# Feed-forward block of a hybrid decoder step on one core: sample rows' high and low parts in one operand, the last two down projections adjacent, and the first weight split moved into the block before

## The reference, cut to what matters

```python
def conv_ffn(hn, conv_buf, p):
    up = hn @ p['w_up']                      # 1024 -> 2 * 2816
    padded = jnp.concatenate([conv_buf.astype(up.dtype), up], axis=1)
    cw = p['conv_w']                         # causal, width 3, over positions
    c = p['conv_b'] + sum(cw[i] * padded[:, i:i + L] for i in range(CONV_W))
    gate, val = jnp.split(c, 2, axis=-1)
    return (jax.nn.silu(gate) * val) @ p['w_down'], padded[:, -(CONV_W - 1):]
...
    h = h + cross_attention(rmsnorm(h, p['norm_x']), mkv, p)
    f, new_conv = conv_ffn(rmsnorm(h, p['norm_ffn']), conv_buf, p)
    return h + f, new_kv, h_re, h_im, new_conv
```

## Time and profile before

| what | value |
|---|---|
| time, median of 3 runs | 2151.79 us (2150.81 to 2152.84) |
| time of the profiled execution | 2154.55 us |
| its span, first to last instruction | 2152.9 us |
| mean granted TensorE clock | 0.896 of full speed |
| PE matmul busy | 1995.6 us (93% of the span) |
| VectorE, ScalarE, GpSimd busy | 965.4, 671.2, 244.8 us |

### The profile page before, as it was taken

The page is one execution under the profiler, slowest core; times in us unless marked ns, Lnnn a source line. Parts: engine busy times, 40 slices in busy tenths (PEclk is TensorE's granted clock), DMA queues, the critical chain, the costliest instruction groups (busy, mean ns, idle before and its releaser), DMA issues. The chain is left out here.

```text
span 2152.9 us, 32099 instructions
## 1 busy us (share of the span) xinstructions
PE 1995.6 (93%) x12704; PEld 1856.9 (86%) x12704; DVE 965.4 (45%) x2020; ACT 671.2 (31%) x1575; POOL 244.8 (11%) x561
## 2 busy tenths in 40 slices
PE   5899999976999599899899898999999999999997
PEld 4798999866789499899899897989988998899886
DVE  5614445447021643644352126355455545554554
ACT  5324333322131532544342104322322232223221
POOL 2502505125100100000000000000000000000000
PEclk9999999955555699999997698999999999999998
DMA  4211100012213242220323310221211121112102
GB/s 139 62 38 43 45 17 21 7 58 89 41 51 106 74 159 69 69 89 1 93 79 104 107 40 20 62 59 32 60 30 58 32 60 30 57 32 60 30 21 82
DMA packets 135728, 125.24 MB, mean 58 GB/s; under 512 B 15284, under 2 KB 128080, under 8 KB 135602
## 3 DMA queue, kind: packets, MB, share of 16 engines
q1 hardware_dynamic: 129986, 109.28, 16.6%
q0 software_dynamic: 5632, 14.44, 2.1%
HBM read 112.43 MB, written 10.60 MB: 57 GB/s over the span
## 5 line engine op out<-in xcount | busy, mean ns | idle before, releaser
L2419 PE MATMUL bank<-XH,WH 128*128 128x352 f32 x1056 | 343.7, 326 | 0.0
L2419 PE MATMUL bank<-XL,WH 128*128 128x352 f32 x1056 | 339.6, 322 | 0.0
L2419 PE MATMUL bank<-XH,WL 128*128 128x352 f32 x1056 | 339.4, 321 | 0.0
L1899 PE MATMUL bank<-WH,XH 128*128 128x256 f32 (+1 forms) x864 | 250.7, 290 | 22.5 <-DVE WL L1795 22.5
L1899 PE MATMUL bank<-WL,XH 128*128 128x256 f32 (+1 forms) x864 | 246.8, 286 | 0.0
L1899 PE MATMUL bank<-WH,XL 128*128 128x256 f32 (+1 forms) x864 | 245.4, 284 | 0.0
L627 PE MATMUL bank<-WH,XH 128*128 128x256 f32 (+3 forms) x648 | 211.5, 326 | 7.7 <-DVE WL L433 7.7
L2350 DVE TENSOR_TENSOR hres<-hres,bank 128x512 f32<-128x512 f32 (+1 forms) x198 | 135.7, 685 | 176.4 <-PE bank L2443 176.2
L627 PE MATMUL bank<-WL,XH 128*128 128x256 f32 (+3 forms) x648 | 203.9, 315 | 0.0
L627 PE MATMUL bank<-WH,XL 128*128 128x256 f32 (+3 forms) x648 | 202.6, 313 | 0.0
L2419 PEld LDWEIGHTS bank<-XH,WH 128*128 128x128 f32 x1056 | 199.2, 189 | 1.2
(11 more groups left out here) (440 smaller groups left out, 3433.8 us busy)
## 6 DMA issues: line engine op xcount, KB each, us to landing
wstage<-w_up SPq DMA_DIRECT2D x44, 512.0 KB, 5.1
ring<-cache_mem_kv SPq DMA_DIRECT2D x64, 256.0 KB, 2.9
dstage<-w_down POOLq DMA_DIRECT2D x22, 512.0 KB
wstage<-w_in SPq DMA_DIRECT2D x10, 1024.0 KB, 5.0
ringS<-cache_kv_dil SPq DMA_DIRECT2D x16, 512.0 KB, 6.9
wstage<-w_xkv SPq DMA_DIRECT2D x8, 1024.0 KB, 5.4
ringS<-cache_kv_dil SPq DMA_DIRECT2D x48, 128.0 KB, 2.7
xin<-x_prompt SPq DMA_DIRECT2D x8, 512.0 KB, 3.5
```

Source lines behind the costliest of these rows:

```text
L1899: ins = nc.tensor.matmul(MM[s % 3][:r, 0:WB], x[:, k, cols], w[:, b % 2, k], start=k == 0 and i == 0, stop=k == KT - 1 and i == 2)
L2419: ins = nc.tensor.matmul(bank[3 * g + j][:, 0:CH], w[:, slot, k, P * g:P * g + P], x[:, k, CH * j:CH * j + CH], start=k == 0 and i == 0, s ...
```

## The change

It has four parts. (1) In `block_dense` "x", the split of the first `w_up` tile into `WH[:, 0]` and `WL[:, 0]` is done at step 32 of 36 (`up_at`) instead of at the start of the feed-forward block; there TensorE starts with the up projection, and the first parameters are transposed after two thirds of its first half. (2) The sample rows' high and low parts of a tile lie side by side in `AS` (64 columns). One matmul with 64 stationary columns and `DH` gives high x high on rows 0 to 31 and low x high on rows 32 to 63; a second, 32 wide, adds high x low. The two row groups are kept apart in `hres` (rows 32 to 63 of the ninth tile) and added once (`fold`) before the last down projection, which is done as before. (3) The parameters of both tiles of a pair lie in one 80-row tile and take one transpose, the last columns of both tiles lie in one 72-column tile and take one transpose. (4) In turn 10 the down projection of pair 9 is moved behind the up projection of tile 21, so that those of pairs 9 and 10 follow each other; the activations and `w_down` parts of tiles 20 and 21 go into the `WH`/`WL` slots that their own up projections have finished with.

```diff
+    up_at = None if has_m else STEPS - 4
...
+            def split_up():
+
+                act.wait_ge(S["w_next"], 64)
+                act.wait_ge(mm, block_end[len(blocks) - 2])
+                nc.scalar.activation(WH[:, 0], wstage[:], ACT.Copy).then_inc(S["u_hi"], 1)
...
+                if s == up_at:
+                    split_up()
...
+            def split_up():
+
+                dve.wait_ge(S["u_hi"], 1)
+                nc.vector.tensor_tensor(WL[:, 0], wstage[:], WH[:, 0].bitcast(F32), ALU.subtract).then_inc(S["u_lo"], 1)
...
-        AH, AL = sb("AH", [P, 2, T], F32R), sb("AL", [P, 2, T], F32R)
+        AH, AL = sb("AH", [P, 2, SEQ], F32R), sb("AL", [P, 2, SEQ], F32R)
+        AS = sb("AS", [P, 4, 2, TS], F32R)
...
-        par = sb("par", [P, 2, P])
-        pT = sb("pT", [P, 2, 2, 20])
-        last = sb("last", [P, 2, 18])
-        co = sb("co", [18, 2, P])
+        par = sb("par", [80, P])
+        pT = sb("pT", [P, 2, 40])
+        last = sb("last", [P, 2, 36])
+        co = sb("co", [72, P])
...
+        w_hi, w_lo, d_hi, d_lo = S["u_hi"], S["u_lo"], sem("d_hi"), sem("d_lo")
...
+        END = TURNS - 1
+
+        def operands(f, slot):
+
+            s = slot
+            if f >= 2 * END:
+                x, w = slice(0, KT // 2), slice(KT // 2, KT)
+                flat = "p k n -> p (k n)"
+                return (WH[:, s, x].rearrange(flat), WL[:, s, x].rearrange(flat), WH[:, s, w].rearrange(flat),
+                        WL[:, s, w].rearrange(flat), AS[:, 2 + s])
+            return AH[:, s], AL[:, s], DH[:, s], DL[:, s], AS[:, s]
...
+            def weights(f):
+                sp.wait_ge(w_lo, f)
+                for g in range(2):
+                    sp.dma_start(wstage[:, :, P * g:P * g + P], w_up[:, :, g, bass.ds(f * P, P)]).then_inc(up_ld, 16)
+
+            def params(n):
+
+                for i in range(2):
+                    cols = bass.ds((n * 2 + i) * P, P)
+                    for lo, hi, src in ((0, 32, I["state_ffn_conv"][0].rearrange("b r (g c) -> (b r g) c", g=2)),
+                                        (32, 38, I["conv_w"][0].rearrange("r (g c) -> (r g) c", g=2)),
+                                        (38, 40, I["conv_b"].rearrange("r (g c) -> (r g) c", g=2))):
+                        sp.dma_start(par[40 * i + lo:40 * i + hi], src[:, cols]).then_inc(par_ld, 16)
+
+            params(0)
+            weights(1)
+            with sp.Fori(1, TURNS) as n:
+                sp.wait_ge(par_p, n)
+                params(n)
+                weights(n * 2)
+                weights(n * 2 + 1)
...
+                nc.scalar.activation(ah, cv[:, 0, 0:SEQ], ACT.Copy)
+                nc.scalar.activation(both[:, 0].rearrange("p (b n) -> p b n", b=DB), tail, ACT.Copy).then_inc(a_hi, 1)
...
+            def add_down(n, lo, hi, wide=True):
 
                 for u in range(lo, hi):
                     t, half = u // 2, u % 2
+                    r = rows(t) if t < NT or not wide else 2 * TS
+                    dst = hres[:r, t, 512 * half:512 * half + 512]
                     dve.wait_ge(dn, n * UNITS + u + 1)
+                    nc.vector.tensor_tensor(dst, dst, bank[6 + u % 2][:r], ALU.add).then_inc(y, 1)
+
+            def fold():
+
+                dve.wait_ge(y, END * UNITS)
+                dve.wait_ge(d_lo, NF)
+                nc.vector.tensor_copy(dstage[0:TS], hres[TS:2 * TS, NT]).then_inc(zero, 1)
+                dve.wait_ge(zero, 2)
+                nc.vector.tensor_tensor(hres[0:TS, NT], hres[0:TS, NT], dstage[0:TS], ALU.add).then_inc(zero, 1)
+                dve.wait_ge(zero, 3)
...
+            f = 2 * END
+            split_up(f + 1, 1)
+            columns_out(END - 1, bank[7], False)
+            for g in range(2):
+                convolve(f, 0, g, 0)
+                convolve(f, 0, g, 1)
+            columns(f, 0, END)
+            cached_columns(f + 1, 1, False, TURNS)
+            product(f)
+            low(f, operands(f, 0))
+            convolve(f + 1, 1, 0, 0)
+            convolve(f + 1, 1, 0, 1)
+            add_down(END - 1, 0, 2)
+            convolve(f + 1, 1, 1, 0)
+            add_down(END - 1, 2, 3)
+            convolve(f + 1, 1, 1, 1)
+            columns(f + 1, 1, None)
+            add_down(END - 1, 3, 6)
+            product(f + 1)
+            add_down(END - 1, 6, 9)
+            low(f + 1, operands(f + 1, 1))
+            add_down(END - 1, 9, UNITS)
+            columns_out(END, bank[0], False)
+            fold()
+            add_down(END, 0, UNITS, False)
...
+            def params(n):
+                pe.wait_ge(par_ld, n * 96 + 96)
+                nc.tensor.transpose(bank[6][:, 0:80], par[:], ident[:80, :80]).then_inc(par_p, 1)
...
-            def columns_out(f):
-                pe.wait_ge(lst, f + 1)
-                for g in range(2):
-                    ins = nc.tensor.transpose(bank[7][0:18, P * g:P * g + P], last[:, g], ident[:])
-                ins.then_inc(co_p, 1)
-
-            def down_project(n):
+            def columns_out(n, dst):
+                pe.wait_ge(lst, n * 2 + 2)
+                nc.tensor.transpose(dst[0:72, 0:P], last[:].rearrange("p i r -> p (i r)"), ident[:]).then_inc(co_p, 1)
+
+            def down_project(n, sources, wide):
                 pe.wait_ge(a_lo, n * 2 + 2)
                 pe.wait_ge(d_lo, n * 2 + 2)
-                pe.wait_ge(co_c, n * 2 + 2)
                 for u in range(UNITS):
                     t, half = u // 2, u % 2
-                    r = rows(t)
+                    out = bank[6 + u % 2]
+                    cols = slice(512 * half, 512 * half + 512)
                     if u >= 2:
                         pe.wait_ge(y, n * UNITS + u - 1)
-                    for s in range(2):
-                        for i, (x, w) in enumerate(((AH, DH), (AH, DL), (AL, DH))):
-                            ins = nc.tensor.matmul(bank[6 + u % 2][:r, :], x[:, s, P * t:P * t + r],
-                                                   w[:, s, 512 * half:512 * half + 512],
-                                                   start=s == 0 and i == 0, stop=s == 1 and i == 2)
+                    for s, (ah, al, dh, dl, both) in enumerate(sources):
+                        if t < NT:
+                            a, b = ah[:, P * t:P * t + P], al[:, P * t:P * t + P]
+                            terms = [(P, a, dh), (P, a, dl), (P, b, dh)]
+                        elif wide:
+                            terms = [(2 * TS, both.rearrange("p h n -> p (h n)"), dh), (TS, both[:, 0], dl)]
+                            if s:
+                                terms.reverse()
+                        else:
+                            terms = [(TS, both[:, 0], dh), (TS, both[:, 0], dl), (TS, both[:, 1], dh)]
+                        for i, (r, x, w) in enumerate(terms):
+                            ins = nc.tensor.matmul(out[:r, :], x, w[:, cols],
+                                                   start=s == 0 and i == 0, stop=s == 1 and i == len(terms) - 1)
                     ins.then_inc(dn, 1)
...
+                        columns_out(n - 1, bank[7])
...
+                up_project(f, 0, first, first_params if first else nothing, before_down)
                 if not first:
+                    pe.wait_ge(par_c, n + 1)
+                    pe.wait_ge(co_c, n)
+                    down_project(n - 1, [operands(0, 0), operands(1, 1)], True)
+                up_project(f + 1, 1, False, nothing, after_down)
+
+            turn(0, True)
+            with pe.Fori(1, END) as n:
+                turn(n, False)
+            f = 2 * END
+
+            def before_last():
+                columns_out(END - 1, bank[7])
+
+            up_project(f, 0, False, nothing, before_last)
+            up_project(f + 1, 1, False, nothing, nothing)
+            pe.wait_ge(par_c, TURNS)
+            pe.wait_ge(co_c, END)
+            down_project(END - 1, [operands(0, 0), operands(1, 1)], True)
+            pe.wait_ge(ub, 2 * NF - 1)
+            columns_out(END, bank[0])
+            pe.wait_ge(y, END * UNITS)
+            down_project(END, [operands(f, 0), operands(f + 1, 1)], False)
```

More of the change, by code:

```diff
@@ L2209, in _, with split_up @@
             load_down(0)
[L2210 to L2215 removed]
+            pool.wait_ge(d_lo, 1)
+            load_down(1)
+            with pool.Fori(1, TURNS) as n:
+                pool.wait_ge(d_lo, n * 2)
+                load_down(n * 2)
+                store(n - 1, n)
+                pool.wait_ge(d_lo, n * 2 + 1)
+                load_down(n * 2 + 1)
+            store(END, TURNS)
+            pool.wait_ge(co_st, 64 * TURNS)
         @blk.scalar
         def _(act):
[L2219 to L2223 removed]
+            def split_up(f, slot, free):
+                act.wait_ge(up_ld, f * 32)
                 if free:
@@ L2231, in split_down, with tile @@
                     act.wait_ge(dn, free)
-                nc.scalar.activation(DH[:, slot], dstage[:], ACT.Copy).then_inc(d_hi, 1)
-            def tile(f, slot, first, free, more):
```

(32 more changed lines are left out.)

179 lines of the change are left out of this document (64 added, 115 removed).

## The result

The changed kernel takes 2118.83 us (median of 4 runs, 2117.29 to 2120.53). The kernel before, run beside it, takes 2151.30 us (4 runs, 2149.41 to 2152.84). The ratio is 0.9855, with a 95% interval of 0.9843 to 0.9868.

A forecast was written before the change was run, and what follows sets the result against it. TensorE never waits in the loop, so only fewer matmuls or shorter distances between them help there. Terms 9.2 + 6.8 + 9.8 + 1.0 = 26.8 us, taken from 2151.8, gave 2125.0 us; range 2120.5 to 2131.5.

The forecast's parts named there:

- sample rows: Loop down projections: packing drops 40 matmuls at 0.23 us, 9.2 us gained; lower bound 8.2.
- transposes: Loop, between up-projection halves: 63 fewer transposes on TensorE's path at 0.108 us each, 6.8 us gained.
- last two pairs: Loop's end: TensorE's wait before the last down projection and its clock fall go, 9.8 us gained; bounds 7, 12.
- first split and parameters: Feed-forward start: first matmul 5.2 us sooner after a barrier 4.5 us later; term 1.0 us, bounds -0.5 and 4.
- the first rival: Clock holds in dense block, VectorE's queue costs nothing in last pairs: start 2.6, last pairs 11.7, 2121.5 us; chance 0.12.

The follow-up runs named there:

- the layout alone: Kernel before with only AH and AL cut to rows of 1024 and sample rows in AS, matmuls otherwise as before: 2148.26 us, ratio 0.9994.
- the second sitting: Changed kernel run again with nothing edited, beside the kernel before: 2121.14 us, ratio 0.9862.

## Why the prediction was wrong

The forecast was 2125.0, the result 2118.83: 6.2 us. Of these 0.5 are the base (2151.8 against 2151.3 beside the result), and 5.7 the gain, 32.5 instead of 26.8. Two things make up the 5.7. S puts the gain at 30.8, so up to 4.0 us are missing in the sum (2.0 if the kernel before starts its feed-forward block as in the run with the layout alone). The rest, 1.7 us or more, is chance between executions: the second sitting has a gain of 28.9 and a median of 2121.14, which would have been inside the range. That the result fell outside is in part chance; that the sum was too small is not.

| term | predicted | measured | by |
|---|---|---|---|
| sample rows | 9.2 | 8.6 | the run with six matmuls |
| transposes | 6.8 | 6.5 | turns of 71.65 and 71.03 us: 10.5 x 0.62 |
| last two pairs | 9.8 | 11.0 | the run with them apart |
| first split and parameters | 1.0 | 0.5 to 2.5 | from the add of step 27 to the end of the first half of the up projection |
| rows of AH and AL | none | 2.8 | rows of 1024 against 1056 |
| sum | 26.8 | 29.4 to 31.4 | |

S gives 28.8 to 30.8 for the whole. Each row comes from a pair of traces of its own, and together they are 0.6 over it.

**The step that failed** is in the working on the sample rows: it took from the change that a sample unit has four matmuls, and that "all other units have six as before" meant that they cost as before. The sum has no term for them. The same edit shortened the rows of `AH` and `AL` from 1056 to 1024 numbers and so moved three of their four slots. The 96 full-width matmuls in each down projection then stand closer: the median distance is 227 ns instead of 232, the mean 230.8 instead of 233.9 (rows of 1024 and 1056, both with the 512 bytes). The mean is what counts: 10 x 96 x 3.1 ns = 3.0 us, and the runs show 2.8. It is the largest of the pieces that the sum lacked and the only one with no term at all. I had no row for such an effect, and gave the edit neither a price nor a bound; a bound of 2% on the ten down projections' 250 us (5 us) would have let the range hold the result, but I choose that figure only now that the effect is measured.

**Sample rows.** The mechanism was right, and so was the distance. The Trainium skill (TensorE: Matmul & The Clock Gate, section Back-to-back issue gap) gives about 131 ns a matmul of 512 columns in such a stream; the trace does not agree, with 227 ns at a granted clock of 1.00, and 40 matmuls were worth 8.6 us and not 5.2. The 0.6 us short of 9.2 are waits, which I had bounded at 1.0. Waits show in the summary of the down projection's line, in what its engine waited for (us, times):

```profile
its engine sat idle before it (us, times) until:
  DVE hres L2386: 15.0, 37
```

Before it was 5.8 us in 25 waits, and in the run with six matmuls 11.6 us in 27. So the packing adds ten waits, 3.4 us together; that 0.6 us of them are lost and the rest lies beside running matmuls is my reading, not shown one by one.

**Transposes.** The term was right. In two kernels whose loops differ in the transposes alone (the layout alone on the kernel before, and six matmuls in the changed kernel) a turn (from one down projection's start to the next, median) takes 71.65 and 71.03 us. A single transpose costs half of a pair or less: the 80-column one shows as 0.07 us, which I had put at 0.108. The gaps of the chain would add up to 7.3 us (84 x 0.109 less 11 x 0.07 and 10 x 0.11), 0.8 more than the turns show; the turns are the ones to go by.

**Last two pairs.** The path was as described, unit by unit: the down projection of pair 9 took 26.1 us where those of the loop take 24.1, 2.0 lost (1.8 forecast), and 0.7 lay between the two (0.9). Two sizes were off. The slow down projection costs 2.7 us (27.68 against 25.0 in the run with the pairs apart) and not 2.3, and the fold ahead of the first add cost about 0.1 and not 0.7 us. VectorE's timeline:

```profile
2089.53 0.68 DVE L2392 COPY dstage<-hres 32x1024 f32<-32x1024 f32 x1
2090.25 1.21 DVE L2394 TENSOR_TENSOR hres<-hres,dstage 32x1024 f32<-32x1024 f32 x1
2091.49 0.69 DVE L2386 TENSOR_TENSOR hres<-hres,bank 128x512 f32<-128x512 f32 x1
```

The copy takes 0.68 (my bounds 0.3 and 1.2) and the first add ends at 2092.2, just where unit 2 wants its bank (2089.35 + 2.7 = 2092.1). The clock held at 1.00 there.

**First split.** Its parts in the dense block were right: VectorE 2.6 us late (2.8 forecast), the clock fell and cost 1.3 (1.7), the barrier 3.9 us later (4.5), the first matmul within 0.5 us of it. The first matmul then came 1.5 us sooner after the add of step 27 than in the trace of before (41.6 against 43.1), where 0.7 was forecast, and the first half of the up projection was 1.0 shorter (0.3). That is 2.5 for a term of 1.0; but of the same stretch the run with the layout alone took 2.0 less than before with the same instructions, so 0.5 is as possible. The split's own place is worth 0.9.

That the clock fell there in the profiled execution was luck: with the split at step 32 it fell in three traces of nine. The time that this gives back is partly lost again: in the traces in which the clock did not fall at step 33 the first matmul comes 1.3 us sooner, and the slow first up projection takes 0.9 us more for its first 48 matmuls (10.54 against 9.59), so that S differs by only 0.7. The clock's part in the first rival was therefore worth 0.7 and not 1.6. That rival's 2121.5 is the nearest number to the result, but not for its reasons: here the clock fell, and VectorE's queue did cost 2.0 us.

**Open.** Why the distance depends on the place. It is not each matmul's own stationary operand alone: with rows of 1056 slot 0 of `AH` has not moved, and yet the median distance from the first matmul of a unit to the second, which both read it, is 234 ns (227 with rows of 1024), though the means differ by only 1.4 ns. Why the clock falls at one place of the dense block in some traces and not in others. TensorE idles 2.41 to 2.44 us there in all nine; in three (the changed kernel twice, the one with six matmuls) the clock fell 1.2 to 1.4 us after it had resumed, in the other six it held. For example:

```profile
1318.55 1.16 PE L1879 MATMUL bank<-ident,xnx 128*128 128x128 f32 x8 [2.44 <-DVE XL L1831]
```

This is the kernel with 512 bytes ahead of `DH`; its clock shows 1.00 in the windows that follow. The kernel with the last pairs apart, whose instructions are those of the changed kernel up to there, held as well. And where the spread of 7.5 us ahead of step 27 comes from: its add was at 1293.0 to 1300.5 us in the traces.

## What to carry to other kernels

When an edit changes a buffer's shape, price what happens to every instruction that reads it, also those that read as before: 960 matmuls at 3 ns, 2.8 us, outweigh the 0.9 us of a split's place to which I gave most of my working. Price a stream by the mean distance or by its length, not by the median. Where a median of three runs is the base of a sum, carry its spread into the range, and compare traces from a late instruction ahead of the change, after looking at whether the clock took the same course in them. Put extra work where the engine idles anyway (step 27, 2.4 us between adds) and not where the chain has no slack (step 32): same instructions, 3.3 us (2.6 where the clock fell at step 33 in neither).

## What the hardware showed that I had not expected

The distance between two matmuls of 512 columns depends on where the stationary operands lie: at the median 227 ns, and 232 with `AH` and `AL` 128 bytes further (means 230.8 and 234.0); moving `DH` and `DL` by 512 bytes made no difference. A transpose of 80 columns shows as 0.07 us in the chain, one of 128 columns as 0.11. The same instructions passed a wait of TensorE of 2.4 us with the clock falling behind it or holding. One figure for the loads of stationary columns, from the summary of the down projection's line (duration in ns, least, median and most):

```profile
L2511 PEld LDWEIGHTS bank<-DH,AS x40: 132/134/135, 1430.0 to 2087.9; 128*64 128x64 f32 x40
```

64 columns load in 134 ns, 128 in 188 and 32 in 108, all of it under a matmul.
